# Moving the norm-sum matmuls, their square root and one GpSimd subtraction within the input projection of a decoder layer

## The reference

```
u = rms_norm(x, attn_norm_g) @ w_in              # 512 tokens x 3336 columns
u[:RWKV_IN] += (u_prev - u) * mu                 # token shift, 14 column tiles of 128
w, a, g from the low-rank parts of u
kk = k * k_k;  kk = kk / max(sqrt(sum over the head of kk*kk), 1e-12)
r, k, v, kk, decay -> chunked RWKV recurrence
q, k, v of the other heads -> forgetting attention
x = x + mix @ w_out;  x = x + top-4-of-32 expert FFN;  out = rms_norm(x)
```

## Time and profile before

| | |
|---|---|
| median of 3 runs | 1812.91 us (1812.9 to 1813.22) |
| the profiled execution | 1813.22 us, its span 1811.5 us |
| PE busy | 1695.4 us (94% of the span) |
| DVE, ACT, POOL busy | 1371.8, 1052.8, 419.7 us |
| mean granted TensorE clock | 0.954 of full |

### The profile page before, as it was taken

How to read it: one execution, slowest core, us unless ns; L and a number is a source line. 1 busy time by engine, 2 the same in 40 slices (tenths; PEclk the granted TensorE clock), 3 DMA queues, 4 the chain that set the end, 5 groups by cost and what they waited for, 6 DMA issues and landing times.

```text
span 1811.5 us, 24160 instructions
## 1 busy us (share of the span) xinstructions
PE 1695.4 (94%) x8385; PEld 1239.1 (68%) x8385; DVE 1371.8 (76%) x1208; ACT 1052.8 (58%) x928; POOL 419.7 (23%) x276
## 2 busy tenths in 40 slices
PE   6999899898996499999999999999999999999993
PEld 5677787788854267777777767777776777677662
DVE  4499554533335579999999999999999999998893
ACT  4344254323113067777777777777777777777672
POOL 6444222125121401121113112211211131122100
PEclk9999799899997599999999999999999999999996
DMA  5222000200132479999999999999999999999994
GB/s 175 97 70 70 2 1 1 93 1 1 47 118 98 144 264 328 390 374 368 379 383 368 374 376 377 371 380 379 373 362 388 377 369 368 387 381 357 370 365 123
DMA packets 135246, 464.10 MB, mean 256 GB/s; under 512 B 10862, under 2 KB 24220, under 8 KB 135132
## 3 DMA queue, kind: packets, MB, share of 16 engines
q1 hardware_dynamic: 126332, 434.08, 64.2%
q0 software_dynamic: 8144, 26.72, 6.0%
q10 hardware_dynamic: 720, 2.62, 0.4%
HBM read 443.40 MB, written 19.99 MB: 256 GB/s over the span
## 4 chain that ended last, share of the span: by engine, by line
PE 81%; DVE 8%; DMA 5%; ACT 2%; issue 2%; POOL 1%; SPq 0%; DVEq 0%; POOLq 0%; ACTq 0%
PE banks L1441 18%; PE banks L1443 18%; PE banks L1442 18%; DMA slots<-in_expert_w_dram 4%; PE banks L1384 3%; PE banks L1272 2%; PE banks L1282 2%; PE banks L1139 2%; PE banks L1140 2%; PE banks L1141 2%; PE banks L1450 2%; PE banks L1191 1%; DVE lo L1880 1%; PE banks L1470 1%; PE banks L1436 1%
## 5 line engine op out<-in xcount | busy, mean ns | idle before, releaser
L1880 DVE TENSOR_TENSOR lo<-slots,hi 128x2048 fp32r<-128x2048 f32 x384 | 862.7, 2286 | 74.5 <-PE banks L1443 55.3
L956 ACT CAST hi<-slots 128x2048 fp32r<-128x2048 f32 x384 | 734.2, 1913 | 274.2 <-DMA slots<-in_expert_w_dram 143.3
L1441 PE MATMUL banks<-lo,x_hi 128*96 128x512 f32 x1024 | 407.9, 398 | 0.0
L1443 PE MATMUL banks<-hi,x_lo 128*96 128x512 f32 x1024 | 403.6, 394 | 0.0
L1442 PE MATMUL banks<-hi,x_hi 128*96 128x512 f32 x1024 | 402.3, 393 | 0.0
L779 POOL DMA_INDIRECT x_sum<-hT,idy x32 | 103.0, 3219 | 921.5 <-ACT hT L1031 921.5
L1443 PEld LDWEIGHTS banks<-hi,x_lo 128*96 128x96 f32 x1024 | 165.7, 162 | 72.5
L1442 PEld LDWEIGHTS banks<-hi,x_hi 128*96 128x96 f32 x1024 | 166.3, 162 | 67.6
L1441 PEld LDWEIGHTS banks<-lo,x_hi 128*96 128x96 f32 x1024 | 165.9, 162 | 66.9
L1441 PE MATMUL banks<-lo,a_hi 128*96 128x512 f32 x512 | 203.6, 398 | 5.8 <-DVE a_lo L1906 4.1
L1443 PE MATMUL banks<-hi,a_lo 128*96 128x512 f32 x512 | 202.2, 395 | 0.0
(11 more groups left out here) (344 smaller groups left out, 2071.7 us busy)
## 6 DMA issues: line engine op xcount, KB each, us to landing
slots<-in_expert_w_dram SPq DMA_DIRECT2D x384, 1024.0 KB, 10.8
slots<-in_w_in_dram SPq DMA_DIRECT2D x13, 1024.0 KB, 5.1
xs<-in_x_dram SPq DMA_DIRECT2D x8, 512.0 KB, 6.1
slots<-in_w_out_dram SPq DMA_DIRECT2D x2, 2048.0 KB, 8.3
h_rows<-BK ACTq DMA_DIRECT2D x4, 512.0 KB, 6.4
x_sum<-xs SPq DMA_DIRECT2D x4, 512.0 KB, 2.6
xs<-x_sum SPq DMA_DIRECT2D x4, 512.0 KB, 6.5
out_dram<-hT SPq DMA_DIRECT2D x4, 512.0 KB, 2.6
```

Of the source, the lines that this page charges most:

```text
L956: nc.scalar.copy(w_hi[n % HI][:, :, :], raw[r]).then_inc(hi_ready, 1)
L1441: nc.tensor.matmul(out, x_h, w_l, start=first, stop=False)
L1443: return nc.tensor.matmul(out, x_l, w_h, start=False, stop=last)
L1880: tensor_tensor(w_lo[n % LO][:, :, :], raw[n % RAW], w_hi[n % HI][:, :, :], ALU.subtract).then_inc(lo_ready, 1)
```

## The change

Four things are moved; no instruction is added or removed.

- On PE and in the bank plan, the four products "ss" move from after tile 11 (behind the products "g") to after tile 9, ahead of tiles 10 and 11.
- On DVE, taking the sums out (line 1643) moves from after the mix of tile 11 to after that of tile 10.
- On ACT, the four square roots move from after tile 11's exponentials to after tile 16's rounding (of the tile two ahead) and copy.
- On POOL, low part 7 moves ahead of the eight small index operations.

With the new rotation "ss" lies in banks 7, 0, 1, 2, tiles 10 and 11 in 3 and 4, "g" in 5, 6, 7, 0, tile 16 in 1 and tile 17 in 2.

```diff
@@ the bank plan
             if m == 11:
                 for tt in range(TT):
                     rot(("g", tt))
+            if m == 9:
                 for j in range(JT):
                     rot(("ss", j))
@@ GpSimd
-            w_in_low_part(6)
+            for n in range(6, 8):
+                w_in_low_part(n)
             step(nc.gpsimd.iota(iotaEi[:, :], ...
...
-            w_in_low_part(7)
             step(nc.gpsimd.memset(zrow, 0.0))
@@ ScalarE
+                if m == 16:
+                    for j in range(JT):
+                        act.wait_ge(kksum_ready, j + 1)
+                        nc.scalar.activation(AR[:, j, :, 0:C], AR[:, j, :, 0:C], ACT.Sqrt).then_inc(kknorm_ready, 1)
                 if 8 <= m < 8 + JT:
...
-                if m == 11:
-                    for j in range(JT):
-                        act.wait_ge(kksum_ready, j + 1)
-                        nc.scalar.activation(AR[:, j, :, 0:C], AR[:, j, :, 0:C], ACT.Sqrt).then_inc(kknorm_ready, 1)
@@ VectorE
-                if m == 11:
+                if m == 10:
                     for j in range(JT):
                         filled(dve, "ss", j)
```

## The result

The changed kernel takes 1823.49 us in the median of 5 runs (1822.95 to 1828.96), the kernel before 1812.9 us (1808.63 to 1813.22, 5 runs). The ratio is 1.0065, 95% interval 1.0049 to 1.0083. The medians lie 10.6 us apart, and the ratio stands for 11.8 us. The profiled execution took 1823.97 us, its span is 1822.2 us, 10.7 us more than before. The forecast was slower by 7.9 us, 1821 us. The direction and the main wait came out as forecast. The slowdown is a third larger than forecast by the medians and a half larger by the ratio, which would put the changed kernel at 1824.7 us, just past the upper end of the forecast's range (1824.5).

A forecast was written before the change was run, and what follows sets the result against it. Limits: DVE's mixes and scans for m = 4 to 7, then PE alone. PE 6.8 us later, elementwise part 1.1 behind it: +7.9 on the profiled 1813.2 gives 1821.1 us; range 1817 to 1824.5, its own 1819 to 1823.5.

The forecast's parts named there:

- the main wait: Behind tile 9, PE stands waiting for DVE's squares, about 3.4 us and again 4 to 6 us.
- The mechanism on which the forecast rests: PE waits for DVE's squares behind tile 9, with tiles 10, 11 and g queued behind; chance 0.80.
- The products "ss" on PE: Waiting behind tile 9 for the squares, PE ends tile 16 6.8 us later; ends of the term 6.4 and 9.4.
- The last squares: DVE's squares for j = 3 ready at 129.3 us, taking 0.69 instead of 2.71; other bound 131.3.
- The clock: PE's lower clock after the waits behind tile 9 costs 2.0 us, taken between 1.6 and 2.6.
- Banks and low parts: Bank releases for g and tile 16 don't hold PE up; costed at nothing, with 1.6 us of cover.
- The roots and the elementwise part: Roots behind tile 16 start DVE's part at 155.5; lasting 48.7 us, it ends at 204.2, 1.1 behind PE.
- GpSimd's low part 7: Moving it first on POOL gains nothing and delays low part 8 to about 76.8; zero, 5 us of cover.
- Behind the bonus product: Stages after the bonus product keep their length; its own clock may shift it up to a microsecond; counted as nothing.
- rival 2: A second stall, at a bank of g or tile 16 or at the roots: 1826.6 us, threshold 1824; chance 0.10.
- Rival 4: DVE's squares come early, so the 2.31 us wait and 1.6 us of low clock go: 1809.3 us; chance 0.05.

The follow-up runs named there:

- run 3: Kernel before with only the sums "ss" moved (PE behind tile 9, DVE behind the mix of tile 10), roots at their old place: ratio 1.0032.
- run 4: Changed kernel without its GpSimd edit: ratio 1.0051 to the kernel before.
- run 6: Kernel before with the sums "ss" moved behind tile 10 instead of tile 9, roots at their old place: ratio 1.0012.
- run 1: Kernel before with the GpSimd edit alone, low part 7 ahead of the eight index operations: ratio 1.0011.
- run 12: Kernel before with the forget gate's work later on ACT (behind tile 1) and DVE (behind tile 3's mix), plus the GpSimd edit: ratio 0.9968.
- run 10: Kernel before with forget gate's work later on ACT and DVE, sums and roots behind tile 16: 1803.03 us, ratio 0.9956.
- run 7: Kernel before with the sums on PE behind tile 16 and the roots behind tile 16's copy: ratio 0.9995.
- run 11: Kernel before with GpSimd's low parts 7 and 8 ahead of the index operations, zeroed row and stores: ratio 1.0003.

## Why the forecast's mechanism held, and which step failed

The mechanism on which the forecast rests held; the step that failed is the GpSimd edit, put at nothing, and the price of the clock was set too low.

- **The products "ss" on PE: right.** Two waits behind tile 9, released by the squares, together 7.9 us, shown by runs 3, 4 and 6. The forecast has "some 7" for them; its own terms (3.4 us, and 129.3 less 124.0) add up to 8.7, at full clock, while the third sum ran at the low clock in 2.04 us instead of 0.91. The term was 6.8 us at tile 16; without the GpSimd edit it measures 6.8 in run 4, and run 3 has 7.1 at the bonus product.
- **The last squares: right**, 129.2 against 129.3, by run 6 for the stated reason.
- **The clock: mis-sized.** Forecast 2.0 us, measured 3.2 in the changed kernel, 2.15 and 2.3 in runs 4 and 3. This is 1.2 us of the difference. It lies outside both rows between which the forecast took its 2.0 (1.6 and 2.6).
- **Banks and low parts: right.** No wait ahead of g or tile 16.
- **The roots and the elementwise part: right.** 1.1 us behind PE was forecast; run 4 less run 3 is 1.2. Duration 49.0 against 48.7. VectorE's start follows the end of tile 16 by 3.6 us against 3.5 forecast. The Trainium skill (ScalarE: Activation LUTs, section What ACT_TABLE_LOAD costs) gives 2.66 us for a switch of table, by which it would have been 4.9; the trace has 157.75 - 156.45 = 1.30 us from the load to the root and decides against it here.
- **GpSimd's low part 7: the step that failed.** I wrote "Zero, with 5 us of cover". The cover was PE's for low part 8, and it held. What I did not follow is the other engine that GpSimd's work touches: later operations on POOL block other operations on DVE. There they fell on the forget gate's cast and copy and on the mix of tile 1, 3.06 us more than before, behind which ACT's copy of tile 3 stands without slack (80.56, when the mix ended before, to 80.66, when the copy began), and then the sigmoids. At the start of tile 4 that is 1.66 us in the changed kernel (1.55 from tile 0) and 1.85 in run 1; run 4 against the changed kernel has 1.7 at its end. What stands at the bonus product (2.8 and 2.4) has the clock in it. Run 12 shows the path: with the gate work out of it the same edit costs nothing. The forecast had used this very effect for the squares, and not here.
- **Behind the bonus product: "I count nothing".** In the profiles of the two kernels it came out nearly so (1614.7 us against 1615.2). That is luck: over all the profiles, with the same code there, it lies between 1610.6 us (run 10) and 1617.6 (run 3).

The sum for the changed kernel: 7.9 forecast, 1.65 for the GpSimd edit, 1.2 for the clock and 0.4 for the elementwise part give 11.15, against 207.55 - 196.31 = 11.24.

The range: the forecast's own upper end, 1823.5, takes PE's term at its worst and leaves the elementwise part at 48.7 us. With that at its own worst, 49.6, the terms give 1813.2 + 7.9 + 2.6 (PE's 9.4 less 6.8) + 0.9 = 1824.6.

The rivals: none of them happened as told. The nearest is rival 2, a second stall, but it came ahead of tile 4 and not at a bank or a root. Rival 4 (faster) supposed that the squares could come early; run 7 gets 4.3 us on PE by letting the sums wait instead (tile 4 to tile 16 and the sums take 50.3 us, 46.7 of them to the end of tile 16, against 54.6 before), and keeps 2.6 of them at the bonus product, counted from tile 4, since the elementwise part is then the later one.

## What to carry to other kernels

These rules are drawn from this kernel. A product moved ahead of others in an in-order queue is paid for by all that it passes until its slowest input is there; moved behind them it costs nothing as long as its reader has slack. When work is shifted on GpSimd, follow each of its reads of SBUF onto VectorE's timeline, and ask who waits for the operation that it will then land on: cover on the engine that needs the result is not the only cover wanted. The best gain here (run 10) came from asking the reverse question, which work without a deadline stands ahead of the one operation that others wait for.

## What the runs showed of the hardware that I had not expected

**One block can last through two GpSimd instructions.** A copy of 8 x 512 bf16 values, 0.28 us alone, took 5.50 us in run 1 while two subtractions ran back to back on POOL.

**A GpSimd instruction that only writes stretched a cast too.** The cast of 8 x 512 values that takes 0.41 or 0.42 us alone took 1.13 us in the changed kernel over the zeroed row (0.96 us from 74.56), and 1.14 in runs 1 and 11, each time over the same row. The kernel before has no such meeting.

**The same wait, and either clock behind it.** The 2.31 us ahead of the last sum stand in the kernel before and in runs 1 and 11, behind the same work. Before, the granted clock was 0.50 behind it (137 to 140 us); in runs 1 and 11 it stayed at 1.00 (137 to 143 us). Ahead of tile 3 it is the same: a wait of 2.92 us and then a clock of 0.50 in the kernel before, 2.90 us and then 1.00 in run 1. The last sum shows it in the timeline of PE in run 1, where its two passes take 1.12 us, against 2.08 before:

```profile
140.01 1.12 PE L1167 MATMUL banks<-AR,blk 128*128 128x512 f32 x2 [2.31 <-ACT shiftbuf L881]
```

**The same stretch of code differs by 6 us between kernels that do not touch it.** From the start of the bonus product to the third head normalisation on POOL (the first multiplication by `gst` past 470 us) it takes 289.84 us in the changed kernel, 292.16 in run 4 and 286.10 in run 6:

```profile
497.39 1.04 POOL L730 TENSOR_TENSOR slots<-slots,gst 128x512 f32<-128x512 f32 x1 [33.28 <-DVE gst L1802]
```

The granted clock in it differs. The windows from 205 to 215 us of the changed kernel, run 4 and run 6, in this order:

```profile
205.00:215.00 10.00, 8.24 (x45) 7.44 (x44) 3.44 (x7) 1.73 (x5) 0.00 (x0) 0.69 0.00 0
```

```profile
205.00:215.00 10.00, 10.00 (x52) 9.57 (x54) 1.21 (x3) 1.93 (x4) 0.00 (x0) 0.50 0.00 0
```

```profile
205.00:215.00 10.00, 6.63 (x43) 5.78 (x42) 7.89 (x9) 2.50 (x6) 2.34 (x1) 0.67 0.00 0
```

The bonus product's 32 tiny matmuls take 5.87 us in the first, 6.99 in the second and 3.63 in the third. That the clock makes the whole difference was not tested. It does mean that a single profile's total says little about an edit of 2 us in this kernel; distances between marks inside the stretch that was changed repeat to a few tenths, unless the clock changed between the marks.
